# The scan's inverses on compact diagonal blocks and quarter tiles, and column halves for the small heads

## The reference, cut to what matters

```
    L = jnp.where(strict, jnp.einsum('bhnik,bhnjk->bhnij', k_beta, k) * decay, 0.0)
    eye = jnp.eye(C, dtype=jnp.float32)
    rhs = jnp.concatenate([v_beta, k_beta * jnp.exp(g)[..., None]], -1)
    sol = lax.linalg.triangular_solve(eye + L, rhs, left_side=True, lower=True)
...
        v_new = u_c - jnp.einsum('bhck,bhkv->bhcv', w_c, S)
        o = jnp.einsum('bhck,bhkv->bhcv', qd_c, S) + jnp.einsum('bhij,bhjv->bhiv', qk_c, v_new)
        S = S * jnp.exp(gl_c)[..., None, None] + jnp.einsum('bhck,bhcv->bhkv', kd_c, v_new)
...
        Sa = jnp.einsum('bhvk,bhk->bhv', S, a_t)
        S = S * w_t[:, :, None, :] + Sa[..., None] * b_t[:, :, None, :] + v_t[..., None] * k_t[:, :, None, :]
        return S, jnp.einsum('bhvk,bhk->bhv', S, r_t)
```

## Time and profile before

| | us |
|---|---|
| median of 3 runs | 4326.65 |
| lowest to highest | 4324.95 to 4332.65 |
| profiled execution | 4323.73 |
| its span | 4321.9 |
| PE busy | 4093.2 (95%) |
| PE weight loads busy | 3545.0 (82%) |
| VectorE, ScalarE, GpSimd busy | 2215.2, 1370.7, 1152.9 |

### The profile page before, as it was taken

One profiled execution on the slowest core, in us unless ns is written; L12 is line 12 of the kernel. 1 busy time (PEld: TensorE's weight loads), 2 busy tenths in 40 slices (PEclk: granted clock), 3 DMA queues, 4 the chain that ended last, 5 costly groups with the idle time before them and its releaser, 6 DMA issues. The chain is left out here.

```text
span 4321.9 us, 61238 instructions
## 1 busy us (share of the span) xinstructions
PE 4093.2 (95%) x24576; PEld 3545.0 (82%) x24576; DVE 2215.2 (51%) x3183; ACT 1370.7 (32%) x2213; POOL 1152.9 (27%) x640
## 2 busy tenths in 40 slices
PE   7999886999999998899999999789998899999999
PEld 6888765999999997788888888678886788888887
DVE  5643366666666666643333333566663333333334
ACT  4321364444444443421111111434543311111112
POOL 1121264333333432411111111223331211111113
PEclk8999877999999998999999999799999999999999
DMA  4231594111111113311111111300003211111112
GB/s 128 77 98 63 153 306 161 60 59 51 63 50 60 55 40 132 109 47 39 39 36 34 36 39 39 108 10 7 4 1 114 77 39 39 39 39 39 39 39 97
DMA packets 205554, 288.00 MB, mean 67 GB/s; under 512 B 31216, under 2 KB 148272, under 8 KB 205376
## 3 DMA queue, kind: packets, MB, share of 16 engines
q1 hardware_dynamic: 205376, 285.50, 20.1%
HBM read 207.47 MB, written 77.99 MB: 66 GB/s over the span
## 5 line engine op out<-in xcount | busy, mean ns | idle before, releaser
L846 DVE TENSOR_TENSOR top_acc<-top_acc,ffn_down 128x512 f32<-128x512 f32 x600 | 412.2, 687 | 358.6 <-PE ffn_down L111 357.9
L109 PE MATMUL ffn_up<-hT_ffn_high,ffn_w_high 128*128 128x512 f32 (+1 forms) x1536 | 544.3, 354 | 4.9 <-DVE hT_ffn_low L808 4.9
L111 PE MATMUL ffn_up<-hT_ffn_high,ffn_w_low 128*128 128x512 f32 (+1 forms) x1536 | 544.0, 354 | 0.0
L110 PE MATMUL ffn_up<-hT_ffn_low,ffn_w_high 128*128 128x512 f32 (+1 forms) x1536 | 543.9, 354 | 0.0
L109 PE MATMUL ffn_down<-ffn_w_high,ffn_f_high 128*128 128x512 f32 x1280 | 498.6, 390 | 0.0
L110 PE MATMUL ffn_down<-ffn_w_low,ffn_f_high 128*128 128x512 f32 x1280 | 498.3, 389 | 0.0
L111 PE MATMUL ffn_down<-ffn_w_high,ffn_f_low 128*128 128x512 f32 x1280 | 497.9, 389 | 0.0
L835 DVE TENSOR_TENSOR ffn_square<-ffn_relu 128x512 f32<-128x512 f32 (+1 forms) x192 | 146.8, 765 | 640.9 <-ACT ffn_relu L761 640.9
L791 POOL TENSOR_TENSOR ffn_w_low<-up_w_raw,ffn_w_high 128x2048 fp32r<-128x2048 f32 x32 | 147.5, 4610 | 734.1 <-ACT ffn_w_high L767 721.3
L109 PEld LDWEIGHTS ffn_up<-hT_ffn_high,ffn_w_high 128*128 128x128 f32 x1536 | 290.7, 189 | 46.5 <-issue 5.5
L794 POOL TENSOR_TENSOR ffn_w_low<-up_w_raw,ffn_w_high 128x2048 fp32r<-128x2048 f32 x32 | 147.0, 4595 | 671.9 <-ACT ffn_w_high L753 671.9
(11 more groups left out here) (477 smaller groups left out, 8918.6 us busy)
## 6 DMA issues: line engine op xcount, KB each, us to landing
up_w_raw<-in_w_ff SPq DMA_DIRECT2D x64, 1024.0 KB, 5.5
s_tm_both<-prepare_tb SPq DMA_DIRECT2D x20, 512.0 KB, 7.0
s_fm_dir<-prepare_fd SPq DMA_DIRECT2D x20, 512.0 KB, 5.9
scan_tb<-s_tm_both SPq DMA_DIRECT2D x20, 512.0 KB, 3.8
scan_fb<-s_fm_both SPq DMA_DIRECT2D x20, 512.0 KB, 4.7
scan_fd<-s_fm_dir SPq DMA_DIRECT2D x20, 512.0 KB, 5.0
up_w_raw<-s_x SPq DMA_DIRECT2D x20, 512.0 KB, 4.8
top_acc<-in_w_in_even SPq DMA_DIRECT2D x18, 512.0 KB, 5.3
```

The lines of the kernel that those rows point to most:

```text
L109: pe.matmul(out, stationary[0], moving[0], start=start, stop=False)
L110: pe.matmul(out, stationary[0], moving[1], start=False, stop=False)
L111: return pe.matmul(out, stationary[1], moving[0], start=False, stop=stop)
L846: dve.tensor_tensor(a, a, out_of(u), ALU.add).then_inc(added, 1)
```

## The change

At levels 1 to 5 all blocks lie on the diagonal of the two 64-row halves, so X and XT hold nothing in the off-diagonal quarters. The change keeps only the diagonal quarters, 64 columns a head: rows 0 to 63 hold the upper left quarter, rows 64 to 127 the lower right one. `Xp`, `XTp`, `Y` and the inner blocks are halved in width. The level products are made by two 64x64 tiles a head, one per half (`level_y`, `level`), and copies and joins take 256 columns. The masks are still made over all of `NTc`, with a mask of 64 columns repeated. Level 6 reads `NTc` itself and has no mask any more. Since the full inverse is read later as a 128x128 stationary operand, there is a wide tile `XTw` per quad: ScalarE copies the diagonal quarters into it after level 5 (`widen`, `g_widen`, `xt_widen`), `last_join` writes the off-diagonal quarter, the rest is cleared once. The large heads' U has tiles of its own (`U_g`). The first inverse is turned by products with the identity (`turn_first`) instead of transposes. For the small heads, `by_halves` makes each product of `right`, `solve` and `outs` twice, with 64 stationary columns each time; the state's product leaves out the two quarters that belong to no head, and VectorE adds it in two halves.

```diff
-    Xp = [E.sb(f"X{q}", [P, 2, GR, P]) for q in range(Q)]
-    XTp = [E.sb(f"XT{q}", [P, 2, GR, P]) for q in range(Q)]
+    Xp = [E.sb(f"X{q}", [P, 2, GR, HALF]) for q in range(Q)]
+    XTp = [E.sb(f"XT{q}", [P, 2, GR, HALF]) for q in range(Q)]
+    XTw = [E.sb(f"XTw{q}", [P, 2, GR, P]) for q in range(Q)]
+    XT = [XTw[quad[g]][:, slot[g], :, :] for g in range(G)]
...
+            def level_y(q, m, bank, masked):
                 for h in range(GR):
-                    last = pe.transpose(ps[:, 0, h * P:(h + 1) * P], gB[:, h, :], ident[:, :])
-                last.then_inc(s["g_first_turned"], 1)
+                    for part in (LOWER, UPPER):
+                        last = pe.matmul(out_block(bank, h, part), masked[part, h, part], x_halves(q, m, h, part),
+                                         start=True, stop=True)
+                return last
+
+            def level(bank, stationary, moving):
+                for h in range(GR):
+                    for part in (LOWER, UPPER):
+                        last = pe.matmul(out_block(bank, h, part), stationary[part, h, :], moving[part, h, :], start=True, stop=True)
+                return last
...
+            def turn_first(q, bank):
+                for h in range(GR):
+                    for part in (LOWER, UPPER):
+                        last = pe.matmul(out_block(bank, h, part), first_inverse[q][part, h, part], ident[part, part],
+                                         start=True, stop=True)
+                return last
...
                 if m < LAST:
                     if u > 0:
                         pe.wait_ge(s["x_joined"], X_UNITS * i + u)
-                    for h in range(GR):
-                        last = pe.matmul(ps[:, 2, h * P:(h + 1) * P], B[u % 2][:, h, :], Y[u % 2][:, h, :],
-                                         start=True, stop=True)
-                    last.then_inc(s["z_product"], 1)
+                    level(2, inner_blocks[1 + u % 2], Y[u % 2]).then_inc(s["z_product"], 1)
...
             def g_solve(i, d):
                 pe.wait_ge(s["gxt_joined"], LAST * i + LAST)
+                pe.wait_ge(s["g_widened"], 2 * i + 2)
...
+            def by_halves(out, stationary, moving, start, stop):
+
+                for part in (LOWER, UPPER):
+                    last = pe.matmul(out[part], stationary[:, part], moving, start=start, stop=stop)
+                return last
...
                 for h in range(GR):
-                    last = pe.matmul(ps[:, g + 2, h * RN:(h + 1) * RN], XT[g][:, h, :], R[g][:, h, :], start=True, stop=True)
+                    last = by_halves(slot_of(g, h), XT[g][:, h, :], R[g][:, h, :], start=True, stop=True)
...
+                    for part, moving in enumerate((U[g], tb[d][:, 2, k * P:(k + 1) * P])):
+                        for a, rows in enumerate((LOWER, UPPER)):
+                            of_head = moving[:, 2 * a + pair, :] if part == 0 else moving[:, rows]
+                            last = pe.matmul(ps[rows, g + 2, 256 + pair * RN:256 + (pair + 1) * RN],
+                                             BK[d][:, part, k * P + a * RN:k * P + (a + 1) * RN], of_head,
+                                             start=(part == 0), stop=(part == 1))
...
                 pe.wait_ge(s["xt_joined"], UNITS * i + UNITS)
+                pe.wait_ge(s["widened"], 4 * i + 4)
                 solve(i, 2)
...
+            def widen(q, made):
+                for part in (LOWER, UPPER):
+                    act.activation(XTw[q][part, :, :, part].rearrange("p a h n -> p (a h) n"),
+                                   XTp[q][part, :, :, :].rearrange("p a h n -> p (a h) n"), ACT.Copy).then_inc(made, 1)
...
                     if u > 0:
                         y_copy(i, u)
+                    if u >= X_UNITS:
+                        xt_widen(i, u - X_UNITS + 1)
...
-                for u in range(9, UNITS):
+                for u in range(9, X_UNITS):
                     mask(i, u)
...
-                    dve.tensor_tensor(x, x, in_halves(heads(ps[:, 2, :]), m), ALU.add).then_inc(s["x_joined"], 1)
+                    dve.tensor_tensor(x, x, in_halves(out_blocks(2), m), ALU.add).then_inc(s["x_joined"], 1)
...
-                link(dve.tensor_tensor(state, state, heads(ps[:, g + 2, 256:512], RN), ALU.add))
+                for a, rows in enumerate((LOWER, UPPER)):
+                    of_head = S_r[d][rows, 2 * half:2 * half + 2, a, :]
+                    link(dve.tensor_tensor(of_head, of_head, heads(ps[rows, g + 2, 256:384], RN), ALU.add))
```

More of the change, by code:

```diff
@@ L1636, in z @@
                 if m < LAST:
-                    for h in range(GR):
-                        last = pe.matmul(ps[:, 3, h * P:(h + 1) * P], Y[u % 2][:, h, :], B[u % 2][:, h, :],
-                                         start=True, stop=True)
-                    last.then_inc(s["zt_product"], 1)
+                    level(3, Y[u % 2], inner_blocks[1 + u % 2]).then_inc(s["zt_product"], 1)
                 else:
@@ L2114, in gx @@
                 x = xt_halves(0, m)
[L2115 removed]
+                dve.tensor_tensor(x, x, in_halves(out_blocks(3), m), ALU.add).then_inc(s["gxt_joined"], 1)
             def b_rows(i, o, d):
```

220 lines of the change are left out of this document (112 added, 108 removed).

## The result

The changed kernel takes 4128.48 us (median of 4 runs, 4126.23 to 4132.61) against 4326.47 us of the kernel before on the same chip (4324.95 to 4332.65): a ratio of 0.9541, 95% interval 0.9524 to 0.9557. That is 198 us less; 217 had been forecast, and 4110 us. The profiled execution's span is 4127.4 us.

A forecast was written before the change was run, and what follows sets the result against it. PE's own instructions were taken to bound the scan; -19.3 + 4.0 - 8.6 + 2.0 = -21.9 us a turn, 197 us over nine intervals, 217 in all, giving 4110 us from 4326.65; range 4065 to 4230.

The forecast's parts named there:

- the 72 to 76 us that the prediction gave as its sign: Length of one turn of the scan that was to show the forecast right.
- (b): PE's changes of tile shape: 20 more runs of quarter tiles a turn at 0.2 us, +4.0 us (+2 to +6).
- (d): Small heads' `right`, `solve`, `outs` in paired column halves: 21.4 to 12.9 us, 8.6 us saved a turn.
- (f): New PE waits for VectorE, before `g_solve`, the next y, `w_sums`, and around `gram`/`k_masks`: +2.0 us a turn (0 to +6).
- (a): Levels 1 to 5: 45 products a turn go from 0.893 to 0.464 us as quarter records, 19.3 us saved.
- The fourth rival: Diagonal quarter products don't overlap while small heads' halves do: -2.9 us a turn, about 4290 us or no gain; chance 0.02.
- the third: Rival: PE can't keep up the quarter rate; at 58 ns a record the turn is 6.4 us longer, 4389 us; chance 0.05.
- (c): Turning the three first inverses by 16 quarter records each (0.69 us) instead of four transposes (0.66 us): nothing.
- (e): Other engines: joins 684 to 419 ns, VectorE 56.4 us a turn, GpSimd three masks fewer, ScalarE's `widen` copies cost nothing.
- Column halves one by one: Rival: small heads' column halves don't pair, 4.3 us lost there; turn gains 10.0 us, about 4226 us; chance 0.17.
- VectorE deciding more: Rival: VectorE or the chain of copies and joins decides more; turn of 79 us, 4165 us; chance 0.06.
- the 8 that were to show this rival: More than 8 us of PE idle a turn before joins was to show that VectorE decides.

The follow-up runs named there:

- the fifth run: Changed kernel without the level masks: GpSimd writes only two columns of each block and Y's products read a cleared tile; 4115.23 us, ratio 0.9513.
- the tenth: Changed kernel with the state's scaling moved behind unit 3's joins and, in the large heads' outputs, the bank-freeing operation ahead of the two-SBUF addition; 4118.15 us.
- the eleventh run: Changed kernel with scaling moved, large heads' outputs reordered, and the last small group's outputs on VectorE behind `k_rows` but ahead of `ar`; 4123.6 us.

## Why the prediction was right, and where its terms were off

**What bounds the kernel.** Right. PE is busy in 95% of the turn. Its busy time fell by 21.6 us a turn and the turn by 19.1; what lies between went into waits. The turn was to be 21.9 us shorter, 74.0 us; at 76.8 it lies just outside the 72 to 76 us that the prediction gave as its sign. The mechanism is the one forecast, and the sizes of (b), (d) and (f) are off.

**(a) The levels.** Right. The products on the diagonal run two at a time at the rate of the earlier trace rows; -19.3 us stands. The fourth rival is out by this, and the third too: runs of 48 records keep 32 ns each, shape changes among them.

**(b) Changes of shape, +4.0.** Too small. A run of 48 records has 1.39 us by the rate alone and takes 1.55 (1059.16 to 1060.71), and a full group next to a run has 0.98 to 0.99 us where the earlier trace rows had 0.89. That is 0.16 + 0.1 = 0.26 us a run in place of 0.2, +5.2 a turn.

**(d) The small heads, -8.6.** Right in kind, and 0.9 us too much. `right` is 3.67 (3.6 forecast), the first two `solve` 1.03 (0.93) and the four `outs` 7.96 (7.3); the other two `solve`, between quarter tiles, take 1.42 with a stall of some 0.4 in it. The sum is 14.1, less the stall 13.7, against 12.9: -7.7. What was left out is the changes of shape around them, 0.1 to 0.15 us each, which (b) counted for the quarters alone. The stall comes in every other turn (0.2 to 0.5 us, with 1.08 us for these two `solve` in the turns between) and makes these turns 76.7 to 77.0 instead of 76.55 us long; the trace names nothing that PE waits for there, and its cause is open.

**(c), (e) The other engines.** The joins (414 ns forecast as 419), the masks and `widen` (at no cost, shown by a run) are right. VectorE has 59.1 us a turn instead of 56.4. The step that failed is that the durations of untouched operations were carried over from the kernel before: those with both operands in SBUF stand still while a GpSimd mask runs, and which of them meets a mask changed with PE's pace.

**(f) The new waits, +2.0.** Their places were named rightly: `g_solve`, the next Y, `w_sums`; the sizes are 0.4, 0.6 and 0.8 us where 0.9, 0.9 and 1.0 stood. The one behind `gram` and `k_masks` came with 0.3 us, ahead of the last level's Y, where 1.2 stood. Not in the list is a wait of 0.5 us ahead of `turn_first`, for GpSimd's `gB`, where (c) had nothing; it stands in every run that has the quarter tiles, and none tests it. The one ahead of the second `g_state`, 0.66 us, was not in the list and is due to the collision of (e), as the fifth run (without masks) and the tenth (another order) show. In all PE waits 3.5 us a turn against 1.1 before, +2.4, and the stall of 0.4.

Sum by what was measured in the turn shown: -19.3 + 5.2 - 7.7 + 2.4 + 0.4 = -19.0; this turn is 19.0 us shorter, the mean of nine 19.1. That it meets so well is in part chance. By the distance between starts the waits cost 4.3 us against 1.4 before, +2.9 (the one ahead of `g_state` 0.93 and not 0.66), and by that half a microsecond of the sum stays without a place. The nine intervals give 172 us of 197 forecast. The rest, the last turn and what lies ahead of the loop, gives 22 of the 194.5 us between the two spans, where 20 were forecast. The 3 us ahead of the loop can't be told from this: the first turn starts at 741.33 here, 744.62 in the kernel before, and between 729 and 747 us in the runs that begin it alike.

**The rivals.** Column halves one by one is refuted by `solve` at 1.03 us and by the run that takes them apart. VectorE deciding more (a turn of 79, 4165 us) is a question of degree: the turn of 76.8 lies between, somewhat nearer to 79 than to the forecast's 74.0, while the time is nearer to 4110. PE's 3.8 us idle are well under the 8 that were to show this rival, and the collisions are the grain of truth in it. The clock stayed at 1.00 in the turns; with idle pieces of at most 0.9 us in the changed kernel it never fell, and the run with `outs` moved showed it fall behind 2.2 us idle out of 4.

## What to carry to other kernels

Where stationary and moved sides are both half empty, cut the product into tiles that leave out what is zero and let them run in pairs; even with operands that are shared along the rows, halving the stationary columns pays where they and not the moved columns set the rate (128 stationary columns cost 111 ns a record with 64 moved ones as with 128). Then count what the shorter PE work does to the others: not only how busy they are, but which of their operations will now lie beside each other. Before reordering, look for a place where the reader that frees PE's bank is behind an operation that can stall; here the longest stall wasn't the one that cost, the one ahead of a signal was.

## What the runs showed of the hardware that was not expected

- PE pairs tiles across the ends of groups: with the two quarters of a head four matmuls (8 records) apart, a run of 48 records takes 2.04 us against 1.55 for neighbours; without partners it would be 2.8 by the rate of 58 ns a record.
- An operation of VectorE with two SBUF inputs that starts inside a GpSimd operation stands still to its end: 1.23 us instead of 0.42, two scalings 3.06 instead of 1.41, and so in all 99 cases of nine turns. A mask that starts 0.3 us or more before the end of such an operation takes 1.4 to 1.7 us instead of 1.27.
- A mere order on VectorE cost 15 us, in part by a longer wait and in part by the clock: PE's 2.2 us idle out of 4 was followed by about 4 us at a granted clock of 0.57; with a wait of 1.6 us at the same place (the eleventh run) it fell in one turn of nine.
